# Value products of four heads in one block, and another order of the index tiles, in a two-layer streaming encoder

## The reference, cut to what matters

```python
q, k, v, qi, ki, wt = split_cols(x @ w_in, A_SPLITS)
s = jnp.einsum('bqhd,bld->bqhl', qi, ki).astype(jnp.float32) * (IDX_DIM ** -0.5)
w = wt.astype(jnp.float32) * (IDX_HEADS ** -0.5)
score = jnp.einsum('bqhl,bqh->bql', jax.nn.relu(s), w)
limit = (q_pos // CHUNK + 1) * CHUNK
adm = jnp.arange(L)[None, :] < limit[:, None]
score = jnp.where(adm[None], score, -jnp.inf)
_, idx = lax.top_k(score, topk)
...
logits = jnp.einsum('bqhgd,bqjhd->bqhgj', q, k_sel).astype(jnp.float32) * (A_HEAD_DIM ** -0.5)
p = jax.nn.softmax(logits, axis=-1).astype(v.dtype)
o = jnp.einsum('bqhgj,bqjhd->bqhgd', p, v_sel)
```

## Time and profile before

| | us |
|---|---|
| median of 3 executions | 3093.91 |
| lowest and highest | 3091.62, 3094.25 |
| the profiled execution, its own time | 3091.74 |
| its span, first to last instruction | 3089.9 |
| PE busy in the span | 2934.8 (95%) |
| DVE busy | 1501.9 (49%) |
| ACT busy | 1000.2 (32%) |
| POOL busy | 699.1 (23%) |
| mean granted TensorE clock | 0.978 |

### The profile page before, as it was taken

How to read it: one execution, slowest core, us unless ns; L and a number is a source line. 1 busy time by engine, 2 the same in 40 slices (tenths; PEclk the granted TensorE clock), 3 DMA queues, 4 the chain that set the end, 5 groups by cost and what they waited for, 6 DMA issues and landing times. The chain is left out here.

```text
span 3089.9 us, 44793 instructions
## 1 busy us (share of the span) xinstructions
PE 2934.8 (95%) x17423; PEld 2672.7 (86%) x17423; DVE 1501.9 (49%) x2566; ACT 1000.2 (32%) x1800; POOL 699.1 (23%) x406
## 2 busy tenths in 40 slices
PE   8899799879999999999999999968999999999998
PEld 8889677559899989899979899967998999989897
DVE  4369699942544443444461255536144444443435
ACT  3377577761311212121230244323131212212122
POOL 2221010101211111221121255544122111111121
PEclk9999899989999999999999999989999999999999
DMA  4421612233201010111104323255311111010111
GB/s 141 106 71 58 171 42 42 43 122 106 69 31 54 27 54 27 54 41 41 54 1 144 103 95 118 72 205 181 107 49 54 41 41 54 27 54 27 54 38 64
DMA packets 196199, 222.90 MB, mean 72 GB/s; under 512 B 27793, under 2 KB 172113, under 8 KB 196066
## 3 DMA queue, kind: packets, MB, share of 16 engines
q1 hardware_dynamic: 155666, 157.13, 16.5%
q10 hardware_dynamic: 40400, 63.97, 6.3%
HBM read 171.11 MB, written 49.95 MB: 72 GB/s over the span
## 5 line engine op out<-in xcount | busy, mean ns | idle before, releaser
L770 DVE TENSOR_TENSOR h<-mlp_dn_acc,h 128x512 f32<-128x512 f32 x576 | 397.5, 691 | 339.5 <-PE mlp_dn_acc L740 339.5
L759 DVE TENSOR_TENSOR mlp_sq<-mlp_relu 128x384 f32<-128x384 f32 x192 | 165.8, 864 | 554.9 <-ACT mlp_relu L663 554.9
L663 ACT ACTIVATE mlp_relu<-mlp_up_acc 128x384 f32<-128x384 f32 x192 | 94.5, 492 | 563.3 <-PE mlp_up_acc L725 563.3
L725 PE MATMUL mlp_up_acc<-end_xT_hi,end_w_hi 128*128 128x384 f32 x768 | 258.1, 336 | 2.3 <-PEq L70 2.3
L725 PE MATMUL mlp_up_acc<-mid_xT_hi,mid_w_hi 128*128 128x384 f32 x768 | 257.6, 335 | 2.3 <-PEq L70 2.3
L725 PE MATMUL mlp_up_acc<-end_xT_hi,end_w_lo 128*128 128x384 f32 x768 | 257.9, 336 | 0.0
L725 PE MATMUL mlp_up_acc<-end_xT_lo,end_w_hi 128*128 128x384 f32 x768 | 257.8, 336 | 0.0
L725 PE MATMUL mlp_up_acc<-mid_xT_lo,mid_w_hi 128*128 128x384 f32 x768 | 257.4, 335 | 0.0
L725 PE MATMUL mlp_up_acc<-mid_xT_hi,mid_w_lo 128*128 128x384 f32 x768 | 257.3, 335 | 0.0
L740 PE MATMUL mlp_dn_acc<-mid_w_hi,mlp_hid_hi 128*128 128x512 f32 x576 | 224.7, 390 | 0.0
L740 PE MATMUL mlp_dn_acc<-mid_w_lo,mlp_hid_hi 128*128 128x512 f32 x576 | 224.5, 390 | 0.0
(11 more groups left out here) (307 smaller groups left out, 7199.6 us busy)
## 6 DMA issues: line engine op xcount, KB each, us to landing
mid_w_raw<-in_ffn_w_up ACTq DMA_DIRECT2D x15, 1024.0 KB, 5.3
mid_w_raw<-in_ffn_w_down ACTq DMA_DIRECT2D x15, 1024.0 KB, 5.0
end_w_raw<-in_ffn_w_up ACTq DMA_DIRECT2D x15, 1024.0 KB, 5.3
end_w_raw<-in_ffn_w_down ACTq DMA_DIRECT2D x15, 1024.0 KB, 4.9
mid_w_raw<-in_b_w_in SPq DMA_DIRECT2D x11, 1024.0 KB, 6.8
proj_w_raw<-in_a_w_in SPq DMA_DIRECT2D x8, 1024.0 KB, 5.9
att_q_in<-qT SPq DMA_DIRECT2D x16, 512.0 KB, 7.5
qT<-proj0b_stage SPq DMA_DIRECT2D x24, 192.0 KB, 1.8
```

What stands on the lines that cost most here:

```text
L663: act.activation(relu[:, u % 2, :], up_acc[:, u % 3, 0:GW], ACT.Relu).then_inc(relu_done, 1)
L725: mm = pe.matmul(up_acc[:, u % 3, 0:GW], w_up_s[a][:, k, j * P:(j + 1) * P], x_s[c][:, k, g * GW:(g + 1) * GW], start=(n == 0), stop=(n == ...
L759: dve.tensor_tensor(sq[:, u % 2, :], relu[:, u % 2, :], relu[:, u % 2, :], ALU.mult)\
L770: dve.tensor_tensor(cols, dn_acc[:, v % 3, :], cols, ALU.add).then_inc(added, 1)
```

## The change

Three things are altered.

The values of a quad are multiplied in one block at step n0 + 6. What follows (ACT's copy, the transpose back, DVE's scaling) stands at n0 + 7, 8 and 9 where it stood at n0 + 9, 10 and 11.

The index tiles are scored in the order 5, 7, 6, 4, 3, 2 where it was 7, 6, 5, 4, 3, 2. `FIRST`, the number of units ahead of the plan, is 4 where it was 6. `before_bits`, the number of index items before the search starts, becomes 24 (three tiles) where it was 16, because tiles 7 and 6 are now second and third.

The planner fills in rounds before every index item of the first part of the plan (there was no such place), and before the index items of the second part it allows DVE 1.2 us where it allowed 0.6.

```diff
-CHOICE = list(range(T0, NT_P))[::-1]
+CHOICE = [5, 7, 6, 4, 3, 2]
...
-        FIRST = 6
+        FIRST = 4
...
-        before_bits = IH * len(SEARCHED)
+        before_bits = IH * (1 + max(NUMBER[t] for t in SEARCHED))
...
             for _ in range(4):
+                dve_time += fill(pe_time + 1.2 - dve_time)
                 more_pe, more_dve = index()
...
             if items:
-                dve_time += fill(pe_time + 0.6 - dve_time)
+                dve_time += fill(pe_time + 1.2 - dve_time)
...
-    VALUES_AT = {quad_at(q) + 6 + 2 * half: (q, half) for q in range(NQ) for half in range(2)}
-    OUT_AT, BACK_AT, FINISH_AT = ({quad_at(q) + later: q for q in range(NQ)} for later in (9, 10, 11))
+    VALUES_AT, OUT_AT, BACK_AT, FINISH_AT = ({quad_at(q) + later: q for q in range(NQ)} for later in (6, 7, 8, 9))
...
-                    for j in range(J * half // 2, J * (half + 1) // 2):
+                    for j in range(J):
...
-                    if half == 1:
-                        mm.then_inc(values_done, 1)
+                    mm.then_inc(values_done, 1)
```

More of the change, by code:

```diff
@@ L784 @@
 T0 = TOPK_P // P
-CHOICE = list(range(T0, NT_P))[::-1]
+CHOICE = [5, 7, 6, 4, 3, 2]
+assert sorted(CHOICE) == list(range(T0, NT_P))
 NUMBER = {t: x for x, t in enumerate(CHOICE)}
@@ L1622, in stream_values, with values @@
                               start=False, stop=True).then_inc(pv_done, 1)
-                def values(q, half):
+                def values(q):
                     n0, (pair, _) = quad_at(q), quad(q)
                     J = tile_at(n0) + 1
-                    if half == 0:
-                        pe.wait_ge(turned_out, bank_of[n0 + GH4 - 1][-1] + 1)
-                        pe.wait_ge(o_done, outs(HEADS // GH4 + q - 1))
-                        if q == 0:
-                            pe.wait_ge(v_loaded, 16)
-                    for j in range(J * half // 2, J * (half + 1) // 2):
+                    pe.wait_ge(turned_out, bank_of[n0 + GH4 - 1][-1] + 1)
+                    pe.wait_ge(o_done, outs(HEADS // GH4 + q - 1))
+                    if q == 0:
+                        pe.wait_ge(v_loaded, 16)
+                    for j in range(J):
                         for r in range(2):
@@ L1658, in _ @@
                     if n in VALUES_AT:
-                        values(*VALUES_AT[n])
+                        values(VALUES_AT[n])
                     if n in BACK_AT:
```

## The result

The changed kernel takes 3104.18 us (median of 7, 3100.6 to 3107.06) against 3093.91 (median of 7, 3090.26 to 3095.2) before. The ratio is 1.0029, 95% interval 1.002 to 1.0038: slower by about 9 us by the ratio. The forecast was 3089.3, and the range ended at 3097.5. The profiled execution took 3107.06 us (span 3105.3, granted clock 0.975), 15.3 more than the one of before.

The account below looks back on a forecast made before the run. DVE was taken to bound the attention stage up to head 111, PE the projection stage; -3.9 - 0.8 + 0.5 - 0.6 - 0.55 + 0.7 = -4.65 us on 3093.9 gave 3089.3 us, range 3080.5 to 3097.5.

Parts of the forecast that it names:

- What bounds each stage: PE bounds the projection stage; DVE sets the attention stage's pace up to head 111, PE close behind in tiles 7 and 6.
- Heads 94 to 111: Attention stage: 17.9 us of DVE work go, PE's floor limits the gain: -3.9 us, bounds -4.3 and -2.3.
- Heads 30 to 93: Attention stage: rounds 8.0 us shorter, 6.7 given back in waits at four changes of tile: -0.8 us, bounds -8.0 and +3.
- mid-tile: Between the changes of tile, PE's busy time caps the gain in tile 6: +0.5 us.
- Tile 2 and the merged blocks: Four quads of tile 2, where PE is the bound, each save a block start of 0.15 us: -0.6 us.
- The end: Behind the last turn, the finish two steps earlier saves a block start and part of a wait: -0.55 us, bounds 0 and -0.9.
- The projection stage: After 215 us, one hold of DVE's accumulation by POOL may reach PE, 1.6 us at even odds: +0.7 us, bounds -2.4 and +5.3.
- The streams' heads: Counted among the stages outside projection and attention, called untouched: no change expected.
- The second rival: Projection stage turns DVE-bound after 215 us, all four POOL holds reach PE: 12.8 us in place of 0.7, 3101.4 us; chance 0.12.
- The third: Attention stage: long block delays masks, some 0.3 us in each of 13 quads of tiles 7, 6, 4: +4, 3093.3 us; chance 0.18.

Follow-up runs that it names:

- `order_only`: The changed kernel with the values of a quad in two halves again, new tile order and fills kept: 3088.65 us, ratio 0.9976 to the kernel before.
- `merge_only`: The kernel before with only the values of a quad in one block and the steps behind it earlier: 3108.72 us, ratio 1.0048.
- `cover_halves`: The changed kernel with the third quad of each tile in two halves, at n0 + 6 and n0 + 8: 3098.84 us, ratio 1.0013.
- `spread_split`: The changed kernel with ACT's split of queries in four pieces, one behind each of four exponentials: 3098.24 us, ratio 1.0008.
- `order_no_fills`: New tile order and four units ahead, values in halves, the planner's allowances as in the kernel before: 3093.16 us, ratio 0.9999.
- `after`: The changed kernel itself, with all parts of the change: 3104.18 us, ratio 1.0029 to the kernel before.
- `late_halves`: The changed kernel with two halves in the quads of tiles 3, 0 and 2 alone: 3099.43 us, ratio 1.0011.
- `edge_halves`: The changed kernel with the last quad of each tile in two halves, at n0 + 6 and n0 + 8: 3102.72 us, ratio 1.0027.

## Why the prediction was wrong, step by step

**What bounds each stage: right.** DVE sets the pace up to head 93, PE behind it. `order_only`, with the block undone, shows the DVE side of the forecast in the main: from the mask of head 30 to that of head 94 it took 142.8 us in place of 148.4, 5.6 of the 8.0 us.

**Heads 94 to 111: the number by luck.** The sum had -3.9, 3.7 of it in tile 3 and 0.2 in heads 94 and 95. From the mask of head 94 to that of head 112 the time fell from 31.2 to 27.4 us, the very number, but 1.6 of it is in tile 3 and 2.2 in heads 94 and 95, whose two rounds of 1.19 us went in full. Tile 3 fell by 2.9 us in `order_only`. I had taken PE's busy time less 0.6 us as a floor that can nearly be reached. PE was busy 23.98 of 26.11 us and not 23.6 of 24.0; with one block, ACT and DVE stand while PE multiplies, and PE waits for them afterwards.

**Heads 30 to 93: the step that failed.** The sum had -0.8, with 0.5 against it for mid-tile. From the mask of head 30 to that of head 94 the changed kernel took 5.9 us more (154.3 in place of 148.4; the table's 4.8 for tiles 6, 5, 4 and 1 has the gain of heads 94 and 95 in it). The prediction found the place (the logits behind the block at the third step of a tile), the direction and the first wait well: 2.2 us forecast ahead of head 35, 2.32 measured. For the other three it said 1.5, 2.1 and 1.8; they were 3.29, 2.72 and 3.54, with 0.61 and 0.29 more one head earlier at the last two. What it left out stands in the rows of before, 499.21 and 502.52 above: the second half at n0 + 8 is not only work that is moved, it was what PE did while ACT split queries. I costed the block where it arrived and nothing where it left. Taking it away leaves PE idle for 1.8 to 2.3 us, and after three of the four waits the granted clock is at its lower level for 3.4 us, at the very stretch that feeds the late logits. These three are the waits that came out too long. Where the clock stayed up, the long block alone made about what was forecast: 2.32 us for 2.2 ahead of head 35, and in `merge_only`, which saves no DVE work, 1.50, 1.59 and 1.31 for the sum's 1.1, 1.5 and 1.05. So the term that was missing is the lower clock behind PE's new wait, 1.3 us ahead of head 51; the prediction named a clock below 1.00 as something it had no term for. For heads 67 and 83 its share was not measured apart. `cover_halves` and `spread_split` each take PE's wait away, the first by giving the cover back and the second by cutting ACT's split, and win 5 and 6 us; in both the clock is up at all four changes.

**Tile 2 and the merged blocks: the wrong sign.** The end was right: -0.55 in the sum, and from the last mask to the last scaling 6.5 us became 5.8. The sum had -0.6 for tile 2, by PE's view alone: PE ran without a gap, so a saved start of 0.15 us had to count. It was +1.9. The row I read the earlier trace rows also had ACT busy 4.36 of 4.87 us. A long block on PE makes a pause on the second busiest engine, and that had 0.5 us of room.

**The projection stage: a mechanism right, its victim and size wrong.** The sum had +0.7, bounds to +5.3, and the stage grew by 3.6 us: one hold reaches PE, 2.25 us of stop, and the lower clock behind it is the rest. The prediction had even odds for such a hold at 1.6 us and again nothing for the clock. I had looked for it at the accumulations with two inputs. It struck an operation of 0.17 us on two columns, behind which ACT, and behind ACT PE's accumulator, were waiting. It was no question of DVE's room either: it stays with the old allowances (`order_no_fills`), and DVE has 5.6 us idle in the stretch. The Trainium skill, page "SBUF — State Buffer", section "SBUF: two separate sides", says that a VectorE operation in a 2-port mode is locked out as well, and that the lock is held for the whole instruction. The trace agrees on the length: 4.54 us beside POOL's 4.63, and 1.22 beside pieces of 1.3. It doesn't tell in which mode the operation of 4.54 us ran. The prediction named the 2-port mode and did not look for operations that could be in it.

**The streams' heads: open.** They took 70.2 us in place of 67.2, with nothing in the sum for it. Of eleven profiles with the new order the time was 69.0 to 71.6 in nine, 66.9 and 68.0 in two; with the old order 67.2, 66.7 and 69.6. The difference is a wait for keys of the streams, which come by DMA: 2.0 us for one of them. The load that I suspected in front of it is not clearly the cause. So these 3 us may be no effect of the change at all.

**Rivals and range.** The second rival had the right sign by a mechanism that gave 3.6 us where it had 12.8. The third (the long block holds the mask in every quad) was 0.24 us in a quad of tile 6, 0.14 in tile 4 and nothing in tiles 7 and 5 and 1: small, as weighed. No rival had a wait at the changes of tile above what the forecast already had, and so the range ended 7 us short. The bound for heads 30 to 93 was +3 where +5.9 came.

## What to carry to other kernels

Before two pieces of work are put together, cost the place that is left as well as the place where they arrive: look at what the other engines do just there, who waits for the engine that now has nothing, and what its clock does behind the new idle time. On a chain that goes round several engines, a shorter total on one can be worth less than short pieces on all; here, cutting one lump of 1.9 us and one of 4.6 us into four each, with not a microsecond less of work, brought 6 us on the kernel before and some 10 on `order_only`, where the forecast for the whole change was 4.65. A tiny instruction can carry the price of a long one on another engine, so look for holds by what waits behind the held operation, not by its size.

## What the runs showed of the hardware

- A DVE operation on 128x2 elements with one input (0.17 us) was held for 4.54 us by a POOL instruction that had started 0.12 us before it; with POOL's work in four instructions (5.4 us in all there, 17% more) the longest operation of 128x2 was 1.22 us, a COPY_PREDICATED with two inputs that takes 0.16 elsewhere. MAX8 and MATCH_REPLACE8 beside such a piece took 0.90 and 0.94 us, no more than without POOL.
- TensorE's granted clock stood at its lower level for 3.4 us in the trace after PE waits of 2.0 to 2.3 us in the attention stage (three of four; after the one of 1.81 us it stayed up). Over the four profiles with PE waits of 1.8 to 2.4 us at these changes (`after`, `late_halves`, `edge_halves`, `merge_only`) it fell at nine of sixteen, and in `merge_only` stayed up behind 2.05 and 2.10 us; in the other ten, with waits of at most 1.06 us there, it fell at none. In the projection stage, where PE is otherwise busy, a stop of 2.22 to 2.25 us was followed by 3.4 us at the lower level in all eight profiles that have it. At the lower level a 128x384 matmul took 0.52 us in place of 0.34.
